# Score products of two token groups issued together at every second step of an attention kernel

## The chip, the cores and the metric

The kernel runs on one core of a Trainium2 chip. Time is the device time of one execution, in microseconds (us); a kernel's time is the median of its runs.

## What is computed

The reference is one layer of a bidirectional encoder on x (1, 1024, 1024): neighbourhood attention with 16 heads of 64, a layer norm, a squared-ReLU MLP of width 4096 with a sigmoid-gated per-layer embedding, and a second layer norm, all in float32. Cut to what matters:

```python
def neighborhood_attention(x, w_qkv, rpb, w_o):          # 16 rows of 64 tokens, window 8 x 16
    qkv = (x @ w_qkv).reshape(bsz, rows, GRID_W, 3, NA_HEADS, HEAD_DIM)
    q, k, v = qkv[:, :, :, 0] * HEAD_DIM ** -0.5, qkv[:, :, :, 1], qkv[:, :, :, 2]
    def row_block(r):                                     # one row of queries, kh rows of keys
        s = jnp.einsum('bqhd,bakhd->bhqak', q_r, k_b)
        s = jnp.where(col_in[:, None, :], s + bias, -jnp.inf)
        return jnp.einsum('bhqak,bakhd->bqhd', jax.nn.softmax(s, axis=(-2, -1)), v_b)
    return jnp.moveaxis(lax.map(row_block, jnp.arange(rows)), 0, 1).reshape(bsz, seq, D_MODEL) @ w_o

x = layer_norm(DN_ALPHA * x + neighborhood_attention(x, ...), ln1_g, ln1_b)
hid = jnp.square(jax.nn.relu(x @ w_ff1))
ple = jax.nn.sigmoid(x @ w_ple_gate) * (p @ w_ple_proj)
x = layer_norm(DN_ALPHA * x + hid @ w_ff2 + ple, ln2_g, ln2_b)
```

## The kernel before

Every matrix product is made of three products of a high and a low part (`PASSES`), so operands exist twice, `hi` and `lo`. The high part is a copy by ScalarE (or GpSimd), the low part a subtraction by VectorE (or GpSimd).

The attention is staged by pairs of heads, eight pairs (`PAIRS`), each in 16 steps (`UNITS`): a step handles one unit, that is one head of the pair and one group of 128 tokens, with keys from two or three neighbouring groups (256 or 384 columns). TensorE's program is one hand-written order. At step g of the whole sequence (s = g mod 16 within its pair) it issues:

- the scores of unit s (`scores`, matmuls of L1835): K's high part, then K's low part, both against the same q, into one of two banks `score_ps[u % 2]`;
- the transposes of the probabilities of unit s - 2 (`turn_p`, L1819);
- products with V (`weigh_v`, L1858) for the unit of four steps earlier; some steps have none, some two groups;
- six projection products (`project`, L1719), which make Q and K of the pair after. A projection group has 24 products and K's two groups come before Q's two. They run nearly a pair ahead, so the last pair has them only in its steps 0 and 1; from there embedding products (L1895) and transpositions of p (L1877) are spread over its steps.

The other engines follow in lists with the same g, strictly in order. VectorE's round: evacuations held over (last pair only), `add_bias` (L1542 and L1543: score + bias, negated, with the row's extreme; it frees the score bank through `score_done`), `turned_tile` of unit g - 3 (L1524, low part of the transposed probabilities, counter `turned_lo`), `out_sum` (L1555), `evac` (L1428 for Q, L1432 for K: the low parts of a finished projection), and `invert_total` (L1549), which waits for ScalarE's exponential of the same unit. ScalarE's round: `softmax_exp` (L1252), `turned_tile` of unit g - 2 (L1243), `out_low` (L1259), `evac` (L1167). GpSimd multiplies the probabilities by the reciprocal (`normalise`, L1054) and splits weights.

K has to stand twice in the partitions. When VectorE's last low part of K is done (in its round 12), SyncE, which waits for that count, issues four DMAs (`k_twice`, L778) that copy each half to the other 64 partitions. The first scores of the next pair wait for all four (`k_doubled`), and for the first part of Q (`proj_free`). The waits of `scores`:

```python
if u == 0:
    pe.wait_ge(k_doubled, 64 * j + 128)
...
pe.wait_ge(score_done, UNITS * j + (u + 1))
```

`score_done` starts at 2, so unit u waits for the bias pass of unit u - 2. The very first scores are issued ahead of the step loop, in the last of V's products (`v_product(4)`, L1753), once two banks that V's tiles used are free (`v_lo`, counted by L1503).

Of the kernel before, what the change touches and what calls it, by code (L numbers as in the profile page):

```python
# [20 lines left out]
P = 128  # L21
# [4 lines left out]
PAIRS = HEADS // 2  # L26
# [4 lines left out]
GROUPS = T // P  # L31
# [24 lines left out]
UNITS = 2 * GROUPS  # L56
# [6 lines left out]
FILL = PAIR_GROUPS * GROUP_MMS  # L63
STEP_FILL = FILL // UNITS
LAG = 2
AHEAD = FILL - LAG * STEP_FILL
# [12 lines left out]
QUARTER = GROUPS // 2  # L79
# [27 lines left out]
def blocks_of(g):  # L107

    return [d for d in (-1, 0, 1) if 0 <= g + d < GROUPS]
# [296 lines left out]
def attention(nc, S, x, w_qkv, rpb, mask, w_o, p, w_proj, ln_g, ln_b, w_gate):  # L406
# [5 lines left out]
    with ExitStack() as ctx:  # L412
        def sb(name, shape, dt=F32):
            return ctx.enter_context(nc.sbuf_tensor(name, shape, dt))

        def sem(name):
            return ctx.enter_context(nc.semaphore(name))
# [4 lines left out]
        q_st = sb("q_hi_lo", [P, 2, 2, T], F32R)  # L422

        k_st = []
# [33 lines left out]
        score_full = sem("score_full")  # L458
        score_done = sem("score_done")
# [7 lines left out]
        v_lo = sem("v_lo_done")  # L467
# [109 lines left out]
        def w_parts(p, k):  # L577
            return V_PARTS.index((p, k)) + 1
# [4 lines left out]
        def x_sum_parts(p, k):  # L583
            return KC2 * V_SUMS.index(p) + k + 1
# [67 lines left out]
        def low_count(kind, jn, pieces=W_LOWS):  # L652

            return W_LOWS * (2 * jn + kind - 1) + pieces
# [72 lines left out]
        proj_ps, score_ps, tile_ps, out_ps = S.ps[0:2], S.ps[2:4], S.ps[4:6], S.ps[6:8]  # L727
# [978 lines left out]
        def _(pe):  # L1706
            def project(first, last):

                for m in range(first, last):
                    jn, gi, i = m // FILL, m % FILL // GROUP_MMS, m % GROUP_MMS  # L1710
                    kind, t = gi // 2, gi % 2
                    k, (wp, ap) = i // len(PASSES), PASSES[i % len(PASSES)]
                    if i == 0:
                        pe.wait_ge(proj_free, 2 * PAIR_GROUPS * jn + (2 * gi + 2))
                    if jn == 0 and i == 0:
                        pe.wait_ge(w_lo, low_count(Q_, 0))
                    elif jn and t == 0 and i % (GROUP_MMS // W_LOWS) == 0:
                        pe.wait_ge(w_lo, low_count(kind, jn, i * W_LOWS // GROUP_MMS + 1))
                    mm = nc.tensor.matmul(proj_ps[gi % 2][:, :], w[wp][:, kind, k, :],  # L1719
                                          S.act[ap][:, k, t * HALF:(t + 1) * HALF],  # L1720
                                          start=(i == 0), stop=(i == GROUP_MMS - 1))
                    if i == GROUP_MMS - 1:
                        mm.then_inc(proj_full, 1)
# [65 lines left out]
            def v_product(p):  # L1789

                for k, i in [(2 * n + m, i) for n in range(KC2 // 2) for i in range(QUARTER) for m in range(2)]:
                    if p == 4 and (k, i) == (KC2 // 2, QUARTER - 1):
                        pe.wait_ge(v_lo, 2 * QUARTER + 2)
                        scores(0, 0, 0)
                    if i == 0:
                        pe.wait_ge(first_lo, w_parts(p, k))
                        if p in V_SUMS:
                            pe.wait_ge(t_lo, x_sum_parts(p, k))
                    if k == 0:
                        if p == 5:  # L1800
                            if i:
                                pe.wait_ge(proj_free, 4 + 2 * i)
                            else:
                                pe.wait_ge(x3_sum, X_SUMS_3)
                        elif p == 6:
                            pe.wait_ge(v_lo, i + 1)
                        elif p == 4:
                            pe.wait_ge(v_sum, QUARTER + i + 1)
                        else:
                            pe.wait_ge(v_copied, QUARTER * {3: 1, 7: 2}[p] + i + 1)  # L1810
                    v_products(p, i, k)

            def turn_p(j, u):
                pe.wait_ge(prob_ready, UNITS * j + (u + 1))
                pe.wait_ge(turned_lo, UNITS * j + (u + 1))
                if j == 0 and u < 2:
                    pe.wait_ge(v_lo, 3 * QUARTER + u + 1)
                for i in range(len(blocks_of(u % GROUPS))):
                    mm = nc.tensor.transpose(tile_ps[u % 2][:, i * P:(i + 1) * P],  # L1819
                                             prob[:, u % 4, i * P:(i + 1) * P], S.ident[:, :])  # L1820
                mm.then_inc(turned, 1)

            def scores(par, j, u):
                h, g = u // GROUPS, u % GROUPS
                keys = blocks_of(g)
                cols = slice((g + keys[0]) * P, (g + keys[-1] + 1) * P)
                if u == 0:
                    pe.wait_ge(k_doubled, 64 * j + 128)
                if j == 0 and u == GROUPS // 2 - 1:
                    pe.wait_ge(k_second_in, 16 + 64)  # L1830
                if g % (GROUPS // 2) == 0:
                    pe.wait_ge(proj_free, 2 * PAIR_GROUPS * j + (2 * (2 + g // 4) + h + 1 + 4))
                pe.wait_ge(score_done, UNITS * j + (u + 1))
                for part in range(2):
                    mm = nc.tensor.matmul(score_ps[u % 2][:, 0:P * len(keys)], q_st[:, par, h, g * P:(g + 1) * P],  # L1835
                                          k_st[part][:, par, h, cols], start=(part == 0), stop=(part == 1))
                mm.then_inc(score_full, 1)

            def weigh_v(par, j, nth, h, k):

# [104 lines left out]
            for p in V_PRODUCTS[2:]:  # L1945
                v_product(p)
# [4 lines left out]
            for g in range(STEPS):  # L1951
                j, s = divmod(g, UNITS)
                last = g - UNITS * LAST
                if 0 < g < PAIRS * UNITS:
                    scores(j % 2, j, s)
                if 0 <= g - TURN < PAIRS * UNITS:
                    turn_p(*divmod(g - TURN, UNITS))
                for jo, so in pairs_at(g):
                    for h, k in pv_units_at(so):
                        weigh_v(jo % 2, jo, jo // 2, h, k)  # L1960
                project(min(AHEAD + STEP_FILL * g, PAIRS * FILL), min(AHEAD + STEP_FILL * (g + 1), PAIRS * FILL))
                for u in embeds_at(last):
                    embed(u)
                for n in p_turns_at(last):
                    turn_p_rows(n)
                if last in EARLY_PRODUCTS:
                    done = sum(EARLY_PRODUCTS[i] for i in EARLY_PRODUCTS if i < last)
                    early_products(0, done, done + EARLY_PRODUCTS[last])
# [1391 lines left out]
```

## Time and profile before

| | us |
|---|---|
| median of 3 runs | 1212.5 (1211.63 to 1212.59) |
| the profiled execution | 1212.18 |
| its span | 1210.4 |
| TensorE busy | 1198.8 |
| VectorE busy | 860.4 |
| ScalarE busy | 614.6 |

In the rows below times are microseconds, in a timeline measured from the span's start. PE is TensorE's matmul queue, PEld its weight loads, DVE is VectorE, ACT ScalarE, POOL GpSimd, SPq the DMA issues of SyncE; L1835 is line 1835 of the kernel. A matmul's record starts where it enters the array and is longer than its share of the stream, so the distance from one start to the next is what it costs. In brackets stand the idle time ahead of an instruction and what ended it, inferred from semaphores; "issue" is time for which the profile shows no releaser.

### The profile page before, as it was taken

How to read it: one execution, taken by the hardware profiler on the slowest of the kernel's cores; microseconds unless marked ns; L12 is line 12 of the kernel's file. 1: busy time of each engine (PE TensorE's matmuls, PEld its weight loads, DVE VectorE, ACT ScalarE, POOL GpSimd, SP SyncE). 2: the span in 40 equal slices, each digit the busy share in tenths (PEclk: the TensorE clock that was granted, in tenths of full speed). 3: DMA queues.
4: the chain of work that ended last, by engine and by line, in shares of the span. 5: the costliest groups of instructions: out<-in, count | busy, mean ns of one | idle time of the engine just before them, and what ended most of it. 6: DMA issues, size and time to landing. Idle time of an engine off the chain costs nothing.

```text
span 1210.4 us, 17064 instructions
## 1 busy us (share of the span) xinstructions
PE 1198.8 (99%) x5708; PEld 1004.1 (83%) x5708; DVE 860.4 (71%) x1659; ACT 614.6 (51%) x1194; POOL 214.4 (18%) x262
## 2 busy tenths in 40 slices
PE   9999999999999999999999999999999999999997
PEld 7888888888887888888888888888888888888886
DVE  5785666666667668679677777677764565688786
ACT  5654676767767614244444444444454433333571
POOL 1312555555554424100000000000000000000000
PEclk9999999999999999999999999999999999999999
DMA  9669543344444977593555647566579785778533
GB/s 283 179 191 296 141 111 92 77 126 112 110 128 122 293 207 203 179 330 99 201 202 203 228 173 243 184 216 218 181 273 362 278 292 195 278 241 307 182 105 105
DMA packets 172134, 240.46 MB, mean 199 GB/s; under 512 B 12048, under 2 KB 93072, under 8 KB 171664
## 3 DMA queue, kind: packets, MB, share of 16 engines
q1 hardware_dynamic: 170848, 237.14, 59.9%
q0 software_dynamic: 1056, 2.10, 1.0%
q8 instruction: 47, 0.77, 0.3%
q14 instruction: 39, 0.32, 0.1%
q10 hardware_dynamic: 144, 0.13, 0.0%
HBM read 163.17 MB, written 68.87 MB: 192 GB/s over the span
## 4 chain that ended last, share of the span: by engine, by line
PE 94%; DMA 2%; DVE 2%; issue 1%; ACT 1%; SPq 0%; DVEq 0%; ACTq 0%
PE bank L3304 25%; PE bank L3272 25%; PE bank L1719 12%; PE bank L1902 7%; PE bank L3228 6%; PE bank L1753 5%; PE bank L1858 3%; PE bank L1835 3%; PE bank L1819 3%; PE bank L1783 1%; PE bank L1895 1%; DMA ple_embedding<-embedding_place 1%; DMA v_parts<-v_tile_parts 1%; PE bank L331 1%; DMA k_lo_twice<-k_lo_twice 0%
## 5 line engine op out<-in xcount | busy, mean ns | idle before, releaser
L1054 POOL TENSOR_TENSOR probabilities<-probabilities,total_reciprocal 128x384 f32<-128x384 f32 (+1 forms) x128 | 99.0, 774 | 156.6 <-DVE total_reciprocal L1549 156.5
L3272 PE MATMUL bank<-x_combination,weight_parts 128*128 128x512 f32 x504 | 118.5, 389 | 0.0
L1252 ACT ACTIVATE probabilities<-negated_scores,negated_max 128x384 f32<-128x384 f32 (+1 forms) x128 | 75.5, 590 | 82.3 <-DVE negated_max L1543 82.2
L3272 PEld LDWEIGHTS bank<-x_combination,weight_parts 128*128 128x128 f32 x504 | 94.6, 188 | 19.6
L1719 PE MATMUL bank<-act_T_hi,w_qkv_hi 128*128 128x512 f32 x232 | 93.3, 402 | 0.0
L1719 PE MATMUL bank<-act_T_lo,w_qkv_hi 128*128 128x512 f32 x232 | 91.1, 393 | 0.0
L1719 PE MATMUL bank<-act_T_hi,w_qkv_lo 128*128 128x512 f32 x232 | 91.1, 393 | 0.0
L1543 DVE CUSTOM_DVE_ANT_0 negated_scores<-bank,bias_inner 128x384 f32<-128x384 f32 x96 | 53.2, 554 | 47.8 <-issue 47.3
L2630 ACT ACTIVATE hidden_staging<-hidden_staging 128x512 f32<-128x512 f32 x48 | 30.4, 632 | 95.0 <-DVE hidden_staging L2970 95.0
L3272 PE MATMUL bank<-act_T_hi,weight_parts 128*128 128x512 f32 x240 | 77.3, 389 | 0.0
L3304 PE MATMUL bank<-x_combination,hidden_parts_odd 128*128 128x512 f32 (+1 forms) x324 | 73.1, 381 | 0.0
L3304 PE MATMUL bank<-x_combination,weight_parts 128*128 128x512 f32 x312 | 73.0, 389 | 0.0
L3304 PE MATMUL bank<-w_ff_parts,weight_parts_early 128*128 128x512 f32 x312 | 73.0, 389 | 0.0
L3304 PE MATMUL bank<-w_ff_parts,weight_parts 128*128 128x512 f32 x312 | 73.0, 389 | 0.0
L3304 PEld LDWEIGHTS bank<-x_combination,hidden_parts_odd 128*128 128x128 f32 x324 | 59.3, 188 | 11.8
L1524 DVE TENSOR_TENSOR prob_T_lo<-bank,prob_T_hi 128x256 fp32r<-128x256 f32 (+2 forms) x160 | 68.5, 445 | 0.2 <-ACT prob_T_hi L1243 0.2
L3304 PEld LDWEIGHTS bank<-w_ff_parts,weight_parts 128*128 128x128 f32 x312 | 58.6, 188 | 12.2
L3304 PEld LDWEIGHTS bank<-w_ff_parts,weight_parts_early 128*128 128x128 f32 x312 | 58.6, 188 | 12.1
L3304 PEld LDWEIGHTS bank<-x_combination,weight_parts 128*128 128x128 f32 x312 | 58.6, 188 | 12.1
L1243 ACT ACTIVATE prob_T_hi<-bank 128x256 fp32r<-128x256 f32 (+2 forms) x160 | 60.0, 396 | 2.2 <-PE bank L1858 0.9
L1819 PE MATMUL bank<-identity,probabilities 128*128 128x128 f32 x352 | 59.4, 272 | 0.4 <-DVE prob_T_lo L1524 0.4
L2769 DVE TENSOR_TENSOR weight_parts<-weight_raw,weight_parts 128x512 fp32r<-128x512 f32 x51 | 35.1, 690 | 34.4 <-ACT weight_parts L2539 34.4
(296 smaller groups left out, 2985.1 us busy)
## 6 DMA issues: line engine op xcount, KB each, us to landing
hidden_combinations<-hidden_staging SPq DMA_DIRECT2D x112, 256.0 KB, 2.3
w_ff_in<-in_w_ff SPq DMA_DIRECT2D x27, 1024.0 KB, 8.2
weight_raw<-in_w_ff SPq DMA_DIRECT2D x25, 1024.0 KB, 5.4
weight_raw<-hidden_combinations SPq DMA_DIRECT2D x14, 1024.0 KB, 5.5
hidden_in<-hidden_combinations SPq DMA_DIRECT2D x14, 1024.0 KB, 5.9
v_parts<-v_tile_parts SPq DMA_DIRECT2D x16, 512.0 KB, 7.9
v_hi_lo<-v_parts SPq DMA_DIRECT2D x8, 1024.0 KB, 6.7
weight_raw<-in_na_w_qkv SPq DMA_DIRECT2D x14, 512.0 KB, 3.9
```

The source lines that it names most:

```text
L1054: nc.gpsimd.tensor_tensor(prob[:, u % 4, 0:n], prob[:, u % 4, 0:n], recip[:, u % 4:u % 4 + 1].to_broadcast([P, n]), ALU.mult).then_inc(pro ...
L1243: last = nc.scalar.activation(pT_part(pT[0], g, first, count), tile_ps[u % 2][:, at * P:(at + count) * P].rearrange("p (b q) -> p b q", b= ...
L1252: nc.scalar.activation(prob[:, u % 4, 0:n], score[:, u % 2, 0:n], ACT.Exp, scale=-1.0, bias=nmax[:, u % 4:u % 4 + 1], accum_out=total[:, u ...
L1524: last = nc.vector.tensor_tensor(pT_part(pT[1], g, first, count), tile_ps[u % 2][:, at * P:(at + count) * P].rearrange("p (b q) -> p b q", ...
L1543: nc.vector.tensor_tensor_reduce(out=score[:, u % 2, 0:n], in0=score_ps[u % 2][:, 0:n], in1=table, scale=-1.0, scalar=3e38, op0=ALU.add, o ...
L1719: mm = nc.tensor.matmul(proj_ps[gi % 2][:, :], w[wp][:, kind, k, :], S.act[ap][:, k, t * HALF:(t + 1) * HALF], start=(i == 0), stop=(i == ...
L1753: mm = nc.tensor.matmul(bank, x_part[p](ap, k)[:, i * P:(i + 1) * P], (w_high(p), w_low[p])[wp][:, k, :], start=(p in (1, 6, 5) and k == 0 ...
L1819: mm = nc.tensor.transpose(tile_ps[u % 2][:, i * P:(i + 1) * P], prob[:, u % 4, i * P:(i + 1) * P], S.ident[:, :])
L1902: mm = nc.tensor.matmul(S.ps[2 * par + h][:, :], tile(ap, k), wo(wp, k)[:, h * HALF:(h + 1) * HALF], start=(k == 0 and n == 0), stop=(k == ...
L3228: mm = nc.tensor.matmul(bank, x, weights, start=(k == 0 and i == 0 and p in (1, 5, 6)), stop=(k == KH4 - 1 and i == 2), skip_group_check=p ...
L3272: mm = nc.tensor.matmul(bank, w1_part(wp, u, p)[:, k, :], x_part(ap, p, k), start=(k == 0 and n == 0 and p in (1, 5, 6)), stop=(k == KH4 - ...
L3304: mm = nc.tensor.matmul(bank, hid_part(ap, n, t)[:, k, :], weights(wp)[:, k, :], start=(start and k == 0 and i == 0), stop=(stop and k == ...
```

## The change

Scores of two units are issued together, at even steps, as four matmuls: high part of K for the first and the second unit, then low part for the first and the second. The counter `score_full` rises by 2 behind the fourth. They wait for both score banks (`score_done` at u + 2, so the bias pass of unit u - 1). The wait for the second half of the first pair's K stands one step earlier (u of 2 instead of 3). The first group, ahead of the loop, now holds units 0 and 1 and waits for one more tile of V. Projections are dealt out five at even and seven at odd steps instead of six at each. The other engines' programs are unchanged.

```diff
--- before.py
+++ after.py
@@ -1790,8 +1790,8 @@
 
                 for k, i in [(2 * n + m, i) for n in range(KC2 // 2) for i in range(QUARTER) for m in range(2)]:
                     if p == 4 and (k, i) == (KC2 // 2, QUARTER - 1):
-                        pe.wait_ge(v_lo, 2 * QUARTER + 2)
-                        scores(0, 0, 0)
+                        pe.wait_ge(v_lo, 2 * QUARTER + 3)
+                        scores_of_two(0, 0, 0)
                     if i == 0:
                         pe.wait_ge(first_lo, w_parts(p, k))
                         if p in V_SUMS:
@@ -1820,21 +1820,23 @@
                                              prob[:, u % 4, i * P:(i + 1) * P], S.ident[:, :])
                 mm.then_inc(turned, 1)
 
-            def scores(par, j, u):
+            def scores_of_two(par, j, u):
+
                 h, g = u // GROUPS, u % GROUPS
-                keys = blocks_of(g)
-                cols = slice((g + keys[0]) * P, (g + keys[-1] + 1) * P)
                 if u == 0:
                     pe.wait_ge(k_doubled, 64 * j + 128)
-                if j == 0 and u == GROUPS // 2 - 1:
+                if j == 0 and u == GROUPS // 2 - 2:
                     pe.wait_ge(k_second_in, 16 + 64)
                 if g % (GROUPS // 2) == 0:
                     pe.wait_ge(proj_free, 2 * PAIR_GROUPS * j + (2 * (2 + g // 4) + h + 1 + 4))
-                pe.wait_ge(score_done, UNITS * j + (u + 1))
+                pe.wait_ge(score_done, UNITS * j + (u + 2))
                 for part in range(2):
-                    mm = nc.tensor.matmul(score_ps[u % 2][:, 0:P * len(keys)], q_st[:, par, h, g * P:(g + 1) * P],
-                                          k_st[part][:, par, h, cols], start=(part == 0), stop=(part == 1))
-                mm.then_inc(score_full, 1)
+                    for b in range(2):
+                        keys = blocks_of(g + b)
+                        cols = slice((g + b + keys[0]) * P, (g + b + keys[-1] + 1) * P)
+                        mm = nc.tensor.matmul(score_ps[b][:, 0:P * len(keys)], q_st[:, par, h, (g + b) * P:(g + b + 1) * P],
+                                              k_st[part][:, par, h, cols], start=(part == 0), stop=(part == 1))
+                mm.then_inc(score_full, 2)
 
             def weigh_v(par, j, nth, h, k):
 
@@ -1951,14 +1953,14 @@
             for g in range(STEPS):
                 j, s = divmod(g, UNITS)
                 last = g - UNITS * LAST
-                if 0 < g < PAIRS * UNITS:
-                    scores(j % 2, j, s)
+                if g % 2 == 0 and 0 < g < PAIRS * UNITS:
+                    scores_of_two(j % 2, j, s)
                 if 0 <= g - TURN < PAIRS * UNITS:
                     turn_p(*divmod(g - TURN, UNITS))
                 for jo, so in pairs_at(g):
                     for h, k in pv_units_at(so):
                         weigh_v(jo % 2, jo, jo // 2, h, k)
-                project(min(AHEAD + STEP_FILL * g, PAIRS * FILL), min(AHEAD + STEP_FILL * (g + 1), PAIRS * FILL))
+                project(*(min(AHEAD + STEP_FILL * n - n % 2, PAIRS * FILL) for n in (g, g + 1)))
                 for u in embeds_at(last):
                     embed(u)
                 for n in p_turns_at(last):
```

## Rows read from the trace of the kernel before

**Rows 1.** The page, part 1: busy time, share of the span, instructions.

```profile
PE 1198.8 (99%) x5708; PEld 1004.1 (83%) x5708; DVE 860.4 (71%) x1659; ACT 614.6 (51%) x1194; POOL 214.4 (18%) x262
```

**Rows 2.** Stretches: length, busy time per engine, granted clock, DMA share.

```profile
188.00:226.00 38.00, 38.00 (x215) 33.22 (x214) 26.31 (x99) 26.45 (x69) 20.77 (x28) 1.00 0.38 103
...
374.00:398.00 24.00, 22.57 (x130) 18.48 (x130) 19.93 (x61) 18.15 (x44) 10.44 (x15) 1.00 0.40 137
```

**Rows 3.** Line L1835: idle time of its queues until a releaser (us, times).

```profile
  DMA k_lo_twice<-k_lo_twice: 2.5, 8
  DVE q_hi_lo L1428: 1.4, 3
```

**Rows 4.** Timeline of PE, step 12 of pair 2: start, us, engine, line, operation.

```profile
213.11 0.33 PE L1835 MATMUL bank<-k_hi_twice,q_hi_lo 128*128 128x384 f32 x1
213.28 0.33 PE L1835 MATMUL bank<-k_lo_twice,q_hi_lo 128*128 128x384 f32 x1
...
215.17 0.34 PE L1835 MATMUL bank<-k_hi_twice,q_hi_lo 128*128 128x384 f32 x1
```

**Rows 5.** Timeline of VectorE in the same step (idle time before in brackets).

```profile
213.66 0.56 DVE L1543 CUSTOM_DVE_ANT_0 negated_scores<-bank,bias_inner 128x384 f32<-128x384 f32 x1 [1.11 <-issue]
...
214.13 0.55 DVE L1524 TENSOR_TENSOR prob_T_lo<-bank,prob_T_hi 128x384 fp32r<-128x384 f32 x1
214.72 0.69 DVE L1432 TENSOR_TENSOR k_lo_twice<-bank,k_hi_twice 64x512 fp32r<-64x512 f32 x1
```

**Rows 6.** Timeline of SyncE: first and last of the four doubling DMAs.

```profile
215.44 0.47 SPq L778 DMA_DIRECT2D k_hi_twice<-k_hi_twice  x1
...
217.24 1.18 SPq L778 DMA_DIRECT2D k_lo_twice<-k_lo_twice  x1
```

**Rows 7.** Transfers of K's low part: 215 to 223 us, then the whole kernel.

```profile
DMA to landing us min/median/max: 3.8/4.4/4.9
...
DMA to landing us min/median/max: 3.6/4.5/7.5
```

**Rows 8.** Timeline of PE and its weight loads where pair 3 begins.

```profile
221.96 0.39 PE L1719 MATMUL bank<-act_T_hi,w_qkv_lo 128*128 128x512 f32 x1
...
222.18 0.19 PEld L1835 LDWEIGHTS bank<-k_hi_twice,q_hi_lo 128*128 128x128 f32 x1 [0.26 <-DMA k_lo_twice<-k_lo_twice]
222.19 0.39 PE L1835 MATMUL bank<-k_hi_twice,q_hi_lo 128*128 128x256 f32 x1
...
222.41 0.28 PE L1835 MATMUL bank<-k_lo_twice,q_hi_lo 128*128 128x256 f32 x1
```

**Rows 9.** Timeline of VectorE and PE in steps 1 to 4 of the last pair.

```profile
377.83 0.06 DVE L1542 MEMSET spare<- 128x1 f32 x1 [1.01 <-PE bank L1835]
...
380.67 0.55 DVE L1543 CUSTOM_DVE_ANT_0 negated_scores<-bank,bias_inner 128x384 f32<-128x384 f32 x1
...
383.23 0.55 DVE L1543 CUSTOM_DVE_ANT_0 negated_scores<-bank,bias_inner 128x384 f32<-128x384 f32 x1
383.25 0.44 PE L1835 MATMUL bank<-k_hi_twice,q_hi_lo 128*128 128x384 f32 x1 [0.40 <-DVE q_hi_lo L1428]
```

**Rows 10.** The same timeline: the third and the fourth transposition of p.

```profile
392.49 0.60 PE L1877 MATMUL bank<-identity,weight_raw 128*128 128x128 f32 x4
...
394.35 0.63 PE L1877 MATMUL bank<-identity,weight_raw 128*128 128x128 f32 x4 [0.35 <-ACT embedding_place L1280]
```

**Rows 11.** Timeline of VectorE: low parts of V's tiles 8 to 11.

```profile
98.01 2.47 DVE L1503 TENSOR_TENSOR v_tile_parts<-bank,v_tile_parts 128x512 fp32r<-128x512 f32 x4
```

**Rows 12.** Timeline around step 4 of the first pair.

```profile
117.60 0.68 DVE L1428 SCALAR_TENSOR_TENSOR q_hi_lo<-bank,q_hi_lo 64x512 fp32r<-64x512 f32 x1
...
118.33 0.19 PEld L1835 LDWEIGHTS bank<-k_hi_twice,q_hi_lo 128*128 128x128 f32 x1 [0.43 <-DVE q_hi_lo L1428]
```

**Rows 13.** The chain that ended last: products in turn, then in one bank.

```profile
16.33 1.82 PE bank L1753 x8
...
68.39 38.50 PE bank L1753 x168
```

## What the change was expected to do, and why

> **What bounds the kernel now.** The page's busy line comes first: TensorE is busy for 1198.8 us of a span of 1210.4 [rows 1], so only two things can move the time: work of TensorE, or the few places where it waits. The change adds and removes no matmul; it moves score products (L1835) and projection products (L1719). It acts on eight pairs of heads, each a run of 16 steps, between 107 and 425 us. The stretch views say how full these are: in 188 to 226 us TensorE has no idle time at a granted clock of 1.00, with VectorE busy 26.3 of 38 us; in 374 to 398 us, where no projections are left as filler, it is busy 22.57 of 24 [rows 2]. The next question is which wait ends last at the few places where TensorE waits. For the scores' line the source view names two: the DMA that doubles K (2.5 us, 8 times) and VectorE's low part of Q (1.4 us, 3 times) [rows 3]. Both are idle times of the weight-load and matmul queues together; part of each is hidden.
>
> **The K path, which decides.** I follow it in the pair that starts at 222.18 us; six other pair starts (146.54, 184.36, 259.97, 297.92, 336.12, 373.97) look the same. Step 12 of the pair before begins at 213.11 with two score matmuls 0.17 us apart [rows 4]. VectorE waits for them, starts the bias pass at 213.66 (0.55 after the step's start, 0.38 after the second matmul's), runs the low part of the transposed tile (214.13 to 214.68) and only then the last low part of K, 214.72 to 215.41 [rows 5]. The bias row shows 1.11 us idle before it: what holds VectorE here is the scores, not a backlog. SyncE issues the first doubling DMA at 215.44 and the fourth at 217.24 [rows 6]; the slowest lands 4.9 us after issue [rows 7], so at 222.14. The weight load of pair 3's first score starts at 222.18, named as waiting 0.26 us for that DMA, and its matmul needs 0.22 us to the next where columns alone (256) need 0.12 [rows 8]. So K arrives late by a hair today: the load should start with the last projection at 221.96. There is no cushion; whatever delays K's low part delays TensorE one for one.
>
> **Parts of the change.**
>
> (a) Four score matmuls at each even step instead of two at each step. Columns and loads are the same. A 384-column matmul takes 0.17 us of the stream [rows 4]. The counter rises once, behind the fourth, so for an even unit VectorE starts at 3 x 0.174 + 0.38 = 0.90 us after the step's start instead of 0.55: **0.35 later**. Queued behind that bias pass on VectorE are the tile's low part, the evacuations of K and Q and the reciprocal; ScalarE's exponential waits for it too.
>
> (b) Of that, step 12 matters: the last K part ends at 213.11 + 2.30 + 0.35, the DMAs are issued and land 0.35 later, TensorE's own path from step 12 to step 0 holds the same products as before and so still takes 9.08 (213.11 to 222.19). Stall: 0.35 per pair start. Six starts inside the full stretch: 6 x 0.35 = **+2.1**. The seventh (373.97) goes into (e). Bounds: 0 per start if the landing time were set by something other than issue; 0.6 if the landing is in a bad slot (over the whole kernel K's low transfers land 3.6 to 7.5 us after issue, median 4.5 [rows 7]). I take 0.35, the row's own value.
>
> (c) Odd units are ready about 2 us sooner. VectorE can't use all of it: the bias pass of unit 13 stands behind the reciprocal of unit 12, which stands behind that unit's exponential. No one waits for odd units in the full steps, so 0.
>
> (d) Odd steps now open with transposes (L1819), and TensorE must find `turned_lo` of the tile three units back. In step 12, the shortest (2.06 us, 213.11 to 215.17 [rows 4]), the step becomes 2.06 + 0.35 - 0.23 = 2.18; the load of the first transpose wants to start at 1.95; VectorE's low part ends at 1.57 + 0.35 = 1.92 [rows 5]. It just fits. Cost 0, bounds 0 and 0.05 for each short step (two a pair, 16 in all): up to +0.8. The longer steps (2.3 to 2.6) have 0.2 us or more. The new condition on both score banks (`score_done` of unit u - 1) is met about 0.9 us ahead, since that bias pass now runs in the middle of the odd step; 0. Of the 5-and-7 split: group borders fall on even steps and stay where they are, the `w_lo` waits are for pieces finished some three steps before; 0.
>
> (e) The last pair. Without projections VectorE's queue is the bound from 377.8 to 384.3. Today it idles 1.01 us at 377.83 waiting for the score of step 1 [rows 9]; with that score there from step 0 this goes. But the gain is not kept: at step 2 it must wait for four score matmuls (the step starts at 379.68 today, about 380.0 behind the seventh K stall; + 0.9 = 380.9, against 380.67 today [rows 9]). From there it works without a break as before (380.67 to 383.23, 2.56 us), 0.2 to 0.3 later: bias of unit 3 from 383.5. Step 4's scores today start at 383.25, on VectorE's low part of Q [rows 9]; after, they also need the bias pass of unit 3 done, at about 384.0, and are four. What follows them, the transposes held by `prob_T_lo`, ends up 0.2 to 0.3 later than now. At step 7 the second transposition of p comes 1.86 us after the first (392.49, 394.35 [rows 10]), held by ScalarE; the scores that fill part of that gap today (0.23 us) move in front of it. Sum of the last pair, its own K stall included: **+0.4**, bounds -1.0 (the 1.01 is kept) and +1.2.
>
> (f) Start. The first group is now two units and waits for one more freed bank (`v_lo` 11, not 10). The four low parts n = 8 to 11 are one block from 98.01 to 100.48 [rows 11], over 6 us before TensorE gets there: 0. Unit 1's score leaves step 1. At step 4 of the first pair the load waited 0.43 us for Q's low part, 117.60 to 118.28 [rows 12]; its bias pass belongs to the odd unit 3, whose score now comes with step 2, so that part ends near 118.0: **-0.2**, bounds -0.3 and 0.
>
> (g) Alternating banks inside a group of scores. The chain has both patterns for 512 columns: 8 products into four banks in turn in 1.82 us (0.228 each), 168 mostly into one bank in 38.50 (0.229) [rows 13]. No difference; 256 matmuls x +-0.002 is +-0.5.
>
> **Sum** against the profiled execution's own 1212.18 (span 1210.4 and 1.8 around it): 2.1 + 0.4 - 0.2 = +2.3, so 1214.5. The median of the runs shown is 1212.5, 0.3 above that execution: **1214.8**.
>
> **The skill against the rows.** The fourth K transfer takes 4.9 us from issue to landing [rows 7]. The Trainium skill (DMA: Bandwidth & Descriptors, Anatomy of one DMA) gives, for another issue path, some 2.0 us plus bytes over 436 GB/s. For 256 KB that is an estimate of 2.6 us from that page; K would then land near 219.8, the delay of 0.35 would be free and the sum +0.2. The trace does not bear it out here. Second, the granted clock is 1.00 in a stretch whose products already go round eight banks [rows 2]. The Trainium skill (TensorE: Matmul & The Clock Gate, A second HAM failure mode: psum-queue depth-cycling) says that cycling through PSUM banks can make the clock swing between its levels. By that rule more alternation would cost time; the trace speaks against it.
>
> **Rivals.**
> - *K is not late* (15%): the doubling's landing follows its slot in the DMA queues, not its issue, or TensorE's path between steps 12 and 0 grows by itself. For: landing times vary [rows 7]. Against: in seven pairs load start and landing agree within 0.1 us. Then the sum is +0.2: 1212.7.
> - *Odd steps wait* (10%): the fit in (d) fails. Mechanism: VectorE's low part, 0.35 late in every even round, is needed at the head of the next step, where the two scores used to stand in between. It decides once VectorE's round is more than 0.05 us later than I have it. Price: 0.1 us at 56 odd steps is 5.6 on top of the forecast less its last pair: about 1220. For: 0.03 us of margin in the short steps. Against: longer steps have 0.2 us and more.
> - *Faster* (10%): the change does what its order promises. VectorE keeps the 1.01 us in the last pair, K lands in good slots and even the 0.1 us exposed at each of the seven starts goes, and half the score waits at step heads disappear at some 0.02 us each in 64 steps: -1.0 - 0.7 - 0.2 - 1.3 = -3.2, 1209.3. Against: steps with scores at their head show no gap today [rows 4].
>
> **Chances.** Forecast 65%, by itself 1213.3 to 1216.4. Faster and slower are counted beyond 0.2% (2.4 us, about what a measurement of this kernel tells from no change), so the forecast stands on the upper bound, 1214.9, and splits in halves: same 0.33 and slower 0.32. "K not late" adds 0.12 to same and 0.03 to faster; "odd steps" 0.10 to slower; "faster" 0.07 to faster and 0.03 to same. Together 0.10, 0.48, 0.42. The range leaves out most of the odd-step case and of the faster one: 1211.5 to 1217.2.
>
> **What will show it.** Right: at the seven pair starts the load's wait for K's DMA is some 0.6 us instead of 0.26, the step-12 bias pass starts 0.90 after its step, and a full pair takes 38.2 us instead of 37.8. The odd steps open without a gap; VectorE's wait at step 1 of the last pair is gone, a new one stands at step 2. Wrong: pair starts unchanged, pairs no longer than 37.8, or gaps in front of L1819 at odd steps.

## The result, and the profile after

The changed kernel takes 1216.41 us (median of 10 runs) against 1212.55 for the kernel before on the same chip: a ratio of 1.0032, 95% interval 1.0022 to 1.0042. That is 3.9 us, **slower by 0.3%**. The forecast was 1214.8, with 1211.5 to 1217.2 as its range: the time is inside the range, 1.6 above the forecast and at the upper end of the 1213.3 to 1216.4 that the forecast case had by itself. The sign, which stood on the edge of the 0.2% bound, came out on the slower side; the prediction had given 0.48 to "same" and 0.42 to "slower". One execution of the repeat of the changed kernel (below) took 3123.69 us, for a reason that the record doesn't show; it is left out of that kernel's figures.

The page's busy line, which answers to [rows 1]:

```profile
span 1214.4 us, 17064 instructions
PE 1199.9 (99%) x5708; PEld 1003.8 (83%) x5708; DVE 857.7 (71%) x1659; ACT 612.7 (50%) x1194; POOL 214.3 (18%) x262
```

The counts of instructions are those of before; the span grew by 4.0 us and busy TensorE by 1.1. The two stretches of [rows 2], moved by 1 and 3 us, roughly with the work they hold (length, busy time of PE, PEld, DVE, ACT and POOL, granted clock, DMA share, GB/s):

```profile
189.00:227.00 38.00, 37.82 (x212) 32.77 (x212) 25.57 (x97) 25.90 (x69) 20.55 (x28) 1.00 0.39 103
377.00:401.00 24.00, 21.49 (x127) 18.07 (x127) 18.46 (x60) 17.81 (x44) 10.45 (x15) 1.00 0.38 122
```

The clock is 1.00 as before. Idle time has appeared in the full stretch, the pairs in which projections fill every step (38.00 busy before, 37.82 now), and 1.1 us more of it in the last pair (22.57, now 21.49), 0.23 of that at the pair's start. Which wait it is, the view by line shows, first the scores' line (L1837 now, L1835 before), answering to [rows 3]:

```profile
its engine sat idle before it (us, times) until:
  DMA k_lo_twice<-k_lo_twice: 7.1, 14
  DVE q_hi_lo L1428: 1.6, 2
  DVE negated_max L1543: 1.1, 1
```

The DMA that doubles K went from 2.5 us to 7.1, the sum of both queues. Seven of the 14 are weight loads, 5.0 us of it; in the kernel before they came to 2.4.

The K path through the same pair as in [rows 4 to 8], timelines of PE, its weight loads, VectorE and SyncE (start, us, engine, line, operation, idle time before it):

```profile
214.66 0.51 PE L1837 MATMUL bank<-k_hi_twice,q_hi_lo 128*128 128x384 f32 x2
215.01 0.52 PE L1837 MATMUL bank<-k_lo_twice,q_hi_lo 128*128 128x384 f32 x2
...
215.57 0.55 DVE L1543 CUSTOM_DVE_ANT_0 negated_scores<-bank,bias_inner 128x384 f32<-128x384 f32 x1 [1.90 <-issue]
216.05 0.55 DVE L1524 TENSOR_TENSOR prob_T_lo<-bank,prob_T_hi 128x384 fp32r<-128x384 f32 x1
216.63 0.70 DVE L1432 TENSOR_TENSOR k_lo_twice<-bank,k_hi_twice 64x512 fp32r<-64x512 f32 x1
...
217.36 0.47 SPq L778 DMA_DIRECT2D k_hi_twice<-k_hi_twice  x1
...
219.16 1.18 SPq L778 DMA_DIRECT2D k_lo_twice<-k_lo_twice  x1
...
DMA to landing us min/median/max: 3.8/4.3/4.9
...
223.52 0.39 PE L1719 MATMUL bank<-act_T_hi,w_qkv_lo 128*128 128x512 f32 x1
224.09 0.30 PEld L1837 LDWEIGHTS bank<-k_hi_twice,q_hi_lo 128*128 128x128 f32 x2 [0.61 <-DMA k_lo_twice<-k_lo_twice]
224.09 0.56 PE L1837 MATMUL bank<-k_hi_twice,q_hi_lo 128*128 128x256 f32 x2 [0.18 <-DMA k_lo_twice<-k_lo_twice]
```

Read from the step's start: the bias pass begins 0.91 us in (215.57 less 214.66) where it began 0.55 in, K's last low part 1.97 in instead of 1.61, SyncE's first doubling DMA 2.70 instead of 2.33, the fourth 4.50 instead of 4.13. The landing takes 4.9 us from issue as before, and TensorE's weight load, behind a last projection that started at 223.52, waits 0.61 us where it waited 0.26. The matmul queue itself stands still for 0.18 of that. The whole way is 0.36 longer from end to end.

**Where the time went**, by the starts of the steps in the profiled execution (1216.21 us, against 1212.18 of before): 0.8 us had been lost ahead of the first score (107.52, against 106.73), where the two programs are the same but for one more tile of V that is waited for; 2.7 at the seven pair starts (+0.42, 0.41, 0.34, 0.33, 0.45, 0.34 and 0.37 at the start itself; step 4 of the first pair gave 0.12 back, and the other steps of the full stretch differ by 0.06 or less); 0.4 to 0.5 in the last pair, from its step 0 to its step 14 (40.68, now 41.13); 0.1 behind it. These are one execution of each kernel; what a second pair of executions makes of them stands in the part on why.

### The profile page after: what moved, and what is told of

Its sections match the earlier page's. It is cut to its first block, busy times and chain, and to the rows that moved or that the text cites. A ratio compares the mean times of both kernels' runs of the same rounds, so it can differ in the third digit from the quotient of the medians.

```text
span 1214.4 us, 17064 instructions
## 1 busy us (share of the span) xinstructions
PE 1199.9 (99%) x5708; PEld 1003.8 (83%) x5708; DVE 857.7 (71%) x1659; ACT 612.7 (50%) x1194; POOL 214.3 (18%) x262
## 4 chain that ended last, share of the span: by engine, by line
PE 83%; issue 5%; DMA 5%; DVE 4%; SPq 1%; ACT 1%; DVEq 0%; ACTq 0%
PE bank L3306 25%; PE bank L3274 25%; PE bank L1904 7%; PE bank L3230 6%; PE bank L1753 6%; PE bank L1719 6%; DMA k_lo_twice<-k_lo_twice 3%; PE bank L1837 2%; PE bank L1860 2%; PE bank L1819 1%; PE bank L1783 1%; DMA ple_embedding<-embedding_place 1%; DVE prob_T_lo L1524 1%; SPq L778 1%; DVE k_lo_twice L1432 1%
## 5 line engine op out<-in xcount | busy, mean ns | idle before, releaser
L1819 PE MATMUL bank<-identity,probabilities 128*128 128x128 f32 x352 | 59.4, 272 | 0.5 <-POOL probabilities L1054 0.3
```

## Experiments

Each kernel's runs stand beside runs of the kernel before on the same chip (their medians were 1212.55 to 1213.09; the ratios are against those of the same chip). Times of steps are from the profiled execution, counted from the first score's start in it, so that the scatter ahead of it (below) stays out. "Seven starts" is the start of the last pair, "last pair" the time from its step 0 to its step 14, "K wait" what the weight loads at the pair starts waited for the doubling DMA, sum and longest. A ratio of medians on different chips is not used; differences in us between kernels of different chips are good to about the 0.5 us by which the medians of the kernel before differ.

| kernel | median us | ratio to before, 95% | seven starts | last pair | K wait, longest |
|---|---|---|---|---|---|
| before | 1212.55 | | 267.24 | 40.68 | 2.4, 0.6 |
| before again | 1212.40 | 0.9996 (0.9987 to 1.0005) | 267.43 | 41.85 | 2.6, 0.5 |
| after | 1216.41 | 1.0032 (1.0022 to 1.0042) | 269.91 | 41.13 | 5.0, 0.9 |
| after again | 1215.99 | 1.0028 (1.0016 to 1.0039) | 271.44 | 40.79 | 6.5, 1.6 |
| e1, step 12 unit by unit | 1213.04 | 1.0003 (0.9994 to 1.0012) | 267.28 | 40.78 | 2.6, 0.6 |
| e2, all steps unit by unit | 1212.16 | 0.9994 (0.9985 to 1.0003) | 267.48 | 40.13 | 3.0, 0.7 |
| e4, before, step-12 scores late | 1215.86 | 1.0028 (1.0018 to 1.0038) | 270.40 | 41.18 | 5.7, 1.1 |
| e5, after, K's low part first | 1211.21 | 0.9990 (0.9981 to 0.9999) | 266.06 | 40.66 | none |
| e6, before, K's low part first | 1211.47 | 0.9989 (0.9981 to 0.9998) | 266.18 | 41.63 | none |
| e8, after, six and six | 1215.85 | 1.0025 (1.0013 to 1.0036) | 271.03 | 40.62 | 6.4, 1.6 |
| e9, e2 and K's low part first | 1210.46 | 0.9983 (0.9974 to 0.9992) | 265.69 | 40.31 | none |
| e10, after, last pair in single units | 1214.80 | 1.0018 (1.0009 to 1.0027) | 269.84 | 41.47 | 5.0, 0.9 |

**The theory** is the forecast's: the bias pass of step 12 stands ahead of K's last low part on VectorE, so what delays its scores delays K and TensorE, one for one. **The rivals**: K's landing doesn't follow its issue and the time comes from elsewhere; and the order of banks, the odd steps or the five-and-seven split cost TensorE time by themselves.

### Step 12 alone, unit by unit (e1)

The even unit's two matmuls come first again, with a rise of the counter of their own, in step 12 only; the four stay in one group.

```
-                for part in range(2):
-                    for b in range(2):
+                early = u == 12
+                for part, b in ([(0, 0), (1, 0), (0, 1), (1, 1)] if early else [(0, 0), (0, 1), (1, 0), (1, 1)]):
...
-                mm.then_inc(score_full, 2)
+                    if part == 1 and (early or b):
+                        mm.then_inc(score_full, 1 if early else 2)
```

> The changed kernel, but in step 12 of each pair alone the four score matmuls go both parts of the first unit, then both of the second, and the counter rises by one behind each unit; the work is the same. Theory K (what the change costs is the 0.35 us by which the step-12 bias pass, and with it K's low part and its doubling DMAs, come later): the seven pair starts go back to where they were, 7 x 0.38 = 2.7 us gained on the changed kernel, so about 1.0 us above before (1213.6); the load at a pair's start waits about 0.26 us for K's DMA again. Rival O (the loss comes from odd steps that open with transposes, or from the order of the four matmuls in general): 7 of 64 groups change, at most 0.3 us gained, 1216.1.

Measured 1213.04 (ratio 1.0003), 3.4 us less than the change. The pair starts are those of the kernel before again (267.28 and 267.24), and so is the wait for K:

```profile
213.60 0.55 DVE L1543 CUSTOM_DVE_ANT_0 negated_scores<-bank,bias_inner 128x384 f32<-128x384 f32 x1 [1.54 <-issue]
...
214.67 0.69 DVE L1432 TENSOR_TENSOR k_lo_twice<-bank,k_hi_twice 64x512 fp32r<-64x512 f32 x1
...
PEld bank L1837 <- DMA k_lo_twice<-k_lo_twice: 2.6, 7, 0.6
```

The step starts at 213.05: the bias pass is back at 0.55, K's part at 1.62. One step in sixteen, and only the order and the signal of four matmuls in it, holds nearly all of the change's cost. The gain is larger than the 2.7 expected; 2.6 of it stands at the seven starts.

### Every group unit by unit (e2)

The same edit with `early = True`: what is left of the change is the grouping of two units, one bank after the other, and the split.

> The changed kernel, but every pair of score products goes unit by unit, the counter rising behind each unit; the order 'K's high part first for both' is gone everywhere. Theory K: as the run with step 12 alone, 2.7 us gained on the changed kernel, and in the last pair, where VectorE's round is the bound, up to 0.3 more: about 1213.4. Rival (alternating the banks is worth something on TensorE): slower than the run with step 12 alone, by up to 0.5 us.

Measured 1212.16 (0.9994, the interval holds 1), 1.2 below the 1213.4 expected. Against e1 the seven pairs are 0.2 longer and the last pair 0.65 shorter, where up to 0.3 was expected. So the grouping of two units and the split cost nothing, and going round the banks inside a group, which e1 still does in seven of a pair's eight groups and e2 in none, makes no difference in the full pairs that these runs can tell.

### The kernel before with its step-12 scores behind two projections (e4)

This brings the delay into the kernel before, with nothing else of the change.

```
+                ahead = 2 if s == 12 and j < LAST else 0
+                project(AHEAD + STEP_FILL * g, AHEAD + STEP_FILL * g + ahead)
                 if 0 < g < PAIRS * UNITS:
                     scores(j % 2, j, s)
...
-                project(min(AHEAD + STEP_FILL * g, PAIRS * FILL), min(AHEAD + STEP_FILL * (g + 1), PAIRS * FILL))
+                project(min(AHEAD + STEP_FILL * g + ahead, PAIRS * FILL), min(AHEAD + STEP_FILL * (g + 1), PAIRS * FILL))
```

> The kernel before, with one thing moved: in step 12 of each of the first seven pairs two of the six projection products go ahead of the scores instead of behind them. No pairing, no new wait. The step-12 bias pass starts 2 x 0.23 = 0.46 us later. Theory K: 7 x 0.46 = 3.2 us slower than before, 1215.8, all of it at pair starts. Rival (the landing of K's doubling follows the DMA queues, not its issue, or the loss is in the pairing itself): within 0.5 us of before.

Measured 1215.86 (1.0028), and +3.16 us over the seven starts (expected 3.2). K's landing does follow its issue (6.7 to 7.1 us from SyncE's first issue to the load, at all seven starts): the rival falls. At the start that answers to [rows 8]:

```profile
223.42 0.19 PEld L1835 LDWEIGHTS bank<-k_hi_twice,q_hi_lo 128*128 128x128 f32 x1 [0.74 <-DMA k_lo_twice<-k_lo_twice]
...
PEld bank L1835 <- DMA k_lo_twice<-k_lo_twice: 5.7, 7, 1.1
```

The wait grew from 0.26 to 0.74, which is the 0.46 by which two projection products (2 x 0.23) hold the scores back.

### K's last low part ahead of the bias pass (e5, e6, e9)

The other way round: in VectorE's round 12 the evacuation that stood behind the bias pass, and behind the tile's low part, goes in front of both. e5 does it to the changed kernel, e6 to the kernel before, e9 to e2.

```
                     for which in evacs_before(g - 1):
                         evac(*which)
+                    if s == 12:
+                        for which in evacs_behind(g - 1):
+                            evac(*which)
...
-                if g:
+                if g and s != 12:
                     for which in evacs_behind(g - 1):
                         evac(*which)
```

> The changed kernel, with VectorE's last low part of K put ahead of the bias pass in its round 12 (ScalarE's half of it is done by then, 0.2 us after the step's start), so that the doubling DMAs go out some 1.7 us sooner than in the changed kernel. Theory K: the stalls at pair starts vanish altogether, 7 x (0.38 + about 0.1) = 3.4 us gained on the changed kernel: 1213.0, and no wait of a weight load for K's DMA is left. Rival O: at most 0.5 us gained, 1216.

> The kernel before, unpaired, with VectorE's last low part of K ahead of the bias pass in round 12. Theory K: the landing moves some 1.0 us ahead of its need, so all pairs come down to the 37.75 us seen once K was early in the changed kernel; the pair starts of before then gain 267.24 - 266.06 = 1.2 us: 1211.4. Rival (pairing by itself is worth time once K is out of the way): this kernel stays over 1 us above the changed kernel with K's low part first (1211.2), at 1212.3 or more.

> Scores issued two units at a time, but unit by unit with the counter rising behind each, and K's low part first in round 12. Theory K plus the last pair's share: pairs of 37.75 us as with K's low part first alone, and the last pair 0.5 us shorter, as in the run that went unit by unit everywhere: 1210.7. Rival (the two gains are the same one): 1211.2 or above.

e5 measured 1211.21, 5.2 us less than the change where 3.4 was expected, and 0.1% faster than the kernel before (the interval ends at 0.9999). By the profiled executions 3.85 of the gain stands at the seven starts, 0.5 in the last pair and 1.1 ahead of the first score, which the edit doesn't touch: the last of these is scatter. In e5, step 12 starts at 212.35 and pair 3 at 221.45:

```profile
212.13 0.69 DVE L1432 TENSOR_TENSOR k_lo_twice<-bank,k_hi_twice 64x512 fp32r<-64x512 f32 x1 [0.78 <-ACT k_hi_twice L1167]
...
212.85 0.47 SPq L778 DMA_DIRECT2D k_hi_twice<-k_hi_twice  x1
...
213.35 0.56 DVE L1543 CUSTOM_DVE_ANT_0 negated_scores<-bank,bias_inner 128x384 f32<-128x384 f32 x1
...
221.22 0.39 PE L1722 MATMUL bank<-act_T_hi,w_qkv_lo 128*128 128x512 f32 x1
221.45 0.45 PE L1840 MATMUL bank<-k_hi_twice,q_hi_lo 128*128 128x256 f32 x2
```

K's part waits for ScalarE alone and begins 0.22 us ahead of the step; the doubling DMAs follow at 212.85, and at 221.45 the score products come 0.23 behind the last projection, with no wait. All pairs from the second on take 37.75 us. The order of the change is still in it (four scores, then the bias pass), and in the full steps it costs no more than the 0.03 us a pair by which e9, below, is shorter.

e6 shows the same with the kernel before: pairs of 37.71 to 37.78 us from the second on, 1211.47 (0.9989), as expected (1211.4). Its last pair took 0.95 longer, most of it a wait of 0.82 for the embedding. e9 is the best of all, 1210.46 us (1210.7 expected), 0.9983 (0.9974 to 0.9992): by that ratio it beats the kernel before by 2.1 us, and by the medians the change by 6.0, with every pair from the second to the seventh at 37.72 us.

### The split at six and six (e8)

```
-                project(*(min(AHEAD + STEP_FILL * n - n % 2, PAIRS * FILL) for n in (g, g + 1)))
+                project(min(AHEAD + STEP_FILL * g, PAIRS * FILL), min(AHEAD + STEP_FILL * (g + 1), PAIRS * FILL))
```

> The changed kernel with six projection products at every step, as before. Even steps get 0.23 us longer and odd ones shorter; the work is the same. Theory K: two even steps (12 and 14) lie between the step-12 scores and the next pair's start, and two odd ones, so TensorE's path does not change and the stalls stay: 1216.4 within 0.5. Rival O (odd steps wait for VectorE's low part at their head): longer even steps give it 0.23 us more, the time falls by up to 2 us.

Measured 1215.85 (1.0025), 0.6 below the change, at the edge of the 0.5 expected, with intervals that overlap. The pairs take 38.15, 38.20, 38.23 and 38.51 us where the changed kernel's take 38.22, 38.19, 38.26 and 38.52; two took longer, by a longer wait for K at the start behind them: the fifth 39.12 (38.37 in the change; a wait of 1.57), the first 40.63 (40.10; 1.34). The split of projections costs nothing and brings nothing that can be told apart.

### The last pair in single units (e10)

The steps of the last pair call the old `scores` at every step again; the seven pairs ahead of it stay as changed.

```
-                if g % 2 == 0 and 0 < g < PAIRS * UNITS:
+                if j == LAST:
+                    scores(j % 2, j, s)
+                elif g % 2 == 0 and 0 < g < PAIRS * UNITS:
                     scores_of_two(j % 2, j, s)
```

> The changed kernel, but the last pair issues its scores one unit a step, as before. Theory of the prediction (the last pair loses 0.4 us by pairing, since VectorE waits for four matmuls at step 2 and TensorE for a second bias pass at step 4): 0.45 us off the changed kernel, 1215.9, and the last pair's steps 0 to 14 take 40.7 us, not 41.1. Rival (the last pair's loss is a late echo of its late start): 1216.4, steps 0 to 14 stay at 41.1.

Measured 1214.80, 1.6 below the change where 0.45 was expected; the two ratio intervals still overlap. By its steps the last pair goes as in the kernel before up to step 10 (28.38 us from its start; before 28.40, change 28.77): a gain of 0.39. Then this execution waited for the embedding, and steps 0 to 14 took 41.47 us, not the 40.7 expected and not less than the change's 41.13:

```profile
PE bank L1913 <- ACT embedding_place L1280: 0.8, 1, 0.8
```

So the loss of 0.4 up to step 10 is shown to come from the grouping in the last pair. That the last pair as a whole is shorter without the grouping is not shown, and the 1.6 is not located.

**This wait goes with the order of the last pair.** It stands in front of the embedding products some 33 us into the pair. In the repeat of the kernel before (e12) it reads, with ScalarE's copy that TensorE waits for and the store whose landing that copy waits for:

```profile
407.49 0.60 ACT L1280 ACTIVATE embedding_place<-bank 128x512 f32<-128x512 f32 x1 [4.59 <-DMA ple_embedding<-embedding_place]
...
408.14 0.50 PE L1895 MATMUL bank<-act_T_hi 128*128 128x512 f32 x1 [1.11 <-ACT embedding_place L1280]
```

Five of the twelve traces have a last pair in single units: TensorE waits there in four (0.39 in e4, 0.76 in e10, 0.82 in e6, 1.11 in e12) and not in the first execution of the kernel before. Seven have it in groups of two, and none has the wait. So the 40.68 of the first execution is the kernel before at its best: single units take 40.7 to 41.9, the change's order 40.6 to 41.1, unit by unit in groups of two 40.1 to 40.3. Why the store lands later in the one order was not tried.

### Both kernels once more

The change had lost 0.8 us ahead of the first score, where its program is that of before. Does that belong to it?

> The changed kernel once more, unchanged, to see how far the 0.8 us that its profiled execution lost ahead of the first scores (107.52 us, against 106.73 in the kernel before, with the same program up to there) belongs to it or to that one execution. If it belongs to the one execution: first scores between 106.2 and 107.0, the seven pair starts again at some 269.9 us and the last at some 41.1 us behind them, so a median near 1215.7, 3.1 above the kernel before. If something in the changed kernel's program costs it each time: first scores again near 107.5 and 1216.4, 3.9 above.

> The kernel before once more, as a kernel of its own against its own runs, on the same chip: the ratio should be 1.000 within 0.001; the first scores' start in a second profiled execution (106.73 in the first) shows the scatter of the stretch ahead of them, expected within 0.5 us; pair starts 267.2 and last pair 40.7 again within 0.3.

It doesn't: this time the changed kernel's first score comes at 106.99 and the kernel before's at 107.45 (0.7 from its first execution, where 0.5 was expected). Still the changed kernel takes 1215.99 against 1213.09 on that chip, a ratio of 1.0028, and the kernel before against its own runs has 0.9996. The total came out as expected for this case (1215.7, 3.1 above), but not by the parts expected: the seven starts stand at 271.44 and not at 269.9, 4.0 us above the kernel before (267.43), and the last pair of the kernel before took 41.85 where 40.7 was expected, so the change's 40.79 is 1.1 shorter. At the starts:

```profile
147.87 0.30 PEld L1837 LDWEIGHTS bank<-k_hi_twice,q_hi_lo 128*128 128x128 f32 x2 [1.56 <-DMA k_lo_twice<-k_lo_twice]
...
262.91 0.30 PEld L1837 LDWEIGHTS bank<-k_hi_twice,q_hi_lo 128*128 128x128 f32 x2 [1.07 <-DMA k_lo_twice<-k_lo_twice]
301.63 0.30 PEld L1837 LDWEIGHTS bank<-k_hi_twice,q_hi_lo 128*128 128x128 f32 x2 [1.11 <-DMA k_lo_twice<-k_lo_twice]
...
PEld bank L1837 <- DMA k_lo_twice<-k_lo_twice: 6.5, 7, 1.6
```

The other four waits are 0.58 to 0.93, as in the first execution. Ahead of the load at 262.91, SyncE's issues read:

```profile
255.71 0.47 SPq L778 DMA_DIRECT2D k_hi_twice<-k_hi_twice  x1
256.23 1.64 SPq L778 DMA_DIRECT2D k_lo_twice<-k_lo_twice  x1
257.91 0.60 SPq L778 DMA_DIRECT2D k_hi_twice<-k_hi_twice  x1
258.55 0.61 SPq L778 DMA_DIRECT2D k_lo_twice<-k_lo_twice  x1
```

One of the four issues is long each time; mostly it is the last, with no issue behind it that it could hold up (1.18 at 219.16). Here it is the second, and from the first issue to the load it takes 7.20 us (255.71 to 262.91) instead of the 6.73 of 217.36 to 224.09. It was the second once in the kernel before too (1.36 us) and the third once (1.96), but the way from first issue to load was 6.87 and 6.83 there. Ahead of the wait of 1.56 the four issues were as usual (140.19 to 142.05), and still the load came 7.68 us behind the first.

## Why the prediction came out as it did

- **The K path (b)** is right in place and mechanism. 0.91 for the bias pass (0.90 forecast), 0.36 late at the issue (0.35), the load's wait 0.61 (some 0.6), full pairs of 38.2 to 38.5 (38.2). e1 takes the delay away and 3.4 us go; e4 brings one in and 3.2 come. What was off is the **size of the term**: "I take 0.35, the row's own value". Over two executions each, the loads waited 11.5 us in 14 starts with the change and 5.0 before, 0.46 more per start and 3.3 per run instead of 2.45. An ordinary start costs 0.24 to 0.45, and now and then one costs 0.4 to 0.7 more, because K takes longer from SyncE's first issue: over 7.1 us at 3 of the 14 starts in the two executions of the change and at 2 of 7 in e8 (7.43, 7.67), never over 7.07 in the 14 of the kernel before, nor in the 14 of e4 and e10, which issue as late as the change. I had both ends of that (0 to 0.6 "if the landing is in a bad slot") and took the row of one start as the mean of all; the seven starts don't "look the same": in the kernel before their loads wait 0.23 to 0.58.
- **The last pair (e)**, +0.4 with its K stall of 0.35 included, leaves 0.05 for the pair's own steps. In the first pair of executions they cost 0.45, in the second the change is 1.1 shorter. By the traces the change's order costs 0.1 to 0.4 up to step 10 (28.6 to 28.8 us, single units 28.4 to 28.5), and as much or more was given back in four of five comparisons by the wait for the embedding that the single units have. That the whole term is near its forecast in one comparison is luck: the path that decides it, the embedding's store, is not in the prediction. Two lines went as forecast, the gain at step 1 and its loss at step 2; two things cost more:

```profile
380.58 0.63 PE L1879 MATMUL bank<-identity,weight_raw 128*128 128x128 f32 x4 [0.35 <-DVE q_hi_lo L1428]
...
380.67 0.56 DVE L1543 CUSTOM_DVE_ANT_0 negated_scores<-bank,bias_inner 128x384 f32<-128x384 f32 x1
...
384.26 0.55 DVE L1543 CUSTOM_DVE_ANT_0 negated_scores<-bank,bias_inner 128x384 f32<-128x384 f32 x1 [0.76 <-issue]
...
386.82 0.55 DVE L1543 CUSTOM_DVE_ANT_0 negated_scores<-bank,bias_inner 128x384 f32<-128x384 f32 x1
387.52 0.59 PE L1837 MATMUL bank<-k_hi_twice,q_hi_lo 128*128 128x384 f32 x2 [1.12 <-DVE negated_max L1543]
...
398.18 0.63 PE L1879 MATMUL bank<-identity,weight_raw 128*128 128x128 f32 x4 [0.59 <-ACT embedding_place L1280]
```

  Against [rows 9], as forecast: no wait ahead of unit 1's bias pass (380.67), a new one of 0.76 ahead of unit 2's (384.26), and step 4's scores held by unit 3's bias pass (387.52). Not foreseen: the bias pass of unit 0 is late by 0.34 too, Q's low part stands behind it, and the transposition at the end of step 0 waits 0.35 for that (380.58). I had looked at step 2 and not at step 0, which already has this queue. The held scores of step 4, which were forecast, open at 10.09 us into the pair instead of 9.28, but only 0.14 of that 0.8 is left at step 6. Another 0.24 comes back in step 7: the transposition at 398.18 waits 0.59 for ScalarE where it waited 0.35 [rows 10], since the scores that filled part of that gap now stand in front of it. The prediction saw them move and put no cost on it. At step 8 the pair is 0.38 behind, at step 14 0.46.
- **Odd units (c), odd steps (d), the split, the start (f) and the banks (g).** TensorE has no gap in front of L1819 in the full steps, so the narrow fit in (d) held and the rival "odd steps wait" falls (the weight loads of that line stand idle for 11.5 us in all instead of 4.9, hidden behind running matmuls); step 4 of the first pair gained 0.12 (0.2 forecast); e2 and e8 confirm the zeros of (g) and the split.
- **"K is not late"** falls by e4. Its sum of +0.2 was also added up wrongly: the 0.4 of (e) still holds the seventh start's stall of 0.35, so by its own terms it is some -0.15. The Trainium skill (DMA: Bandwidth & Descriptors, Anatomy of one DMA) has a fit for another issue path, from which the prediction estimated 2.6 us for 256 KB. It does not carry over to these copies: the rows show 4.9. The Trainium skill's passage on cycling through PSUM banks (TensorE: Matmul & The Clock Gate, A second HAM failure mode: psum-queue depth-cycling) doesn't show either: the granted clock is 1.00 in the stretches of both kernels and in e2.
- **"Faster"** falls. Its third part, "the 0.1 us exposed at each of the seven starts", was there to be had, but by K's place on VectorE and not by the order of scores: with the wait gone, a pair takes 37.72 instead of 37.82 (e9, e5, e6).
- **The sum.** Forecast +2.3 over the profiled execution; measured +3.9 and, again, +2.9 between the medians of the second pair. Over the two profiled executions of each kernel the change is 3.4 us longer: 3.3 at the seven starts (2.7 and 4.0), -0.3 in the last pair (+0.45 and -1.1), 0.2 ahead of the first score (106.73 and 107.45 before, 107.52 and 106.99 after) and 0.2 behind step 14. The last three are no larger than what single executions scatter; the starts are the change's cost. A single execution agrees with the median of its kernel only to about 1.7 us, so how often a slow start occurs stays open; what makes one slow wasn't tried.

## What to carry to other kernels

When a transfer at the end of a chain lands just as its user needs it, look for what stands ahead of its producer in the queue of an in-order engine: here a bias pass that waits for another engine's result. One change of order on VectorE took the whole wait away (5.2 us off the changed kernel), more than the best order of the matmuls did (4.3, e2). Grouping products of two units under one signal delays the first unit's consumer by the products that now stand ahead of the signal (0.36 us here); keep the group but signal unit by unit. Cost a delay on such a path with the spread of the transfer's issue and landing over all its occurrences, not with the row of one: without a cushion the slow ones count in full. And take a second execution of the kernel before, too, before a few tenths of a microsecond are put down to the change: here the last pair's sign turned over with it.

## What was not expected of the hardware

The four doubling DMAs take 6.7 to 7.1 us from the first issue to the load that they release, but 7.2 to 7.7 at five starts: three of seven in one execution of the change, two of seven in e8, none in the other execution of the change nor in e4 and e10. All five are in kernels that issue them late (5 of 35 starts; none of the 28 of the kernel before, e1 and e2), but lateness is not what it takes. Where K's low part goes first, SyncE issues them earliest, and they are slower still in e5 and e9: by the traces' landing times the last one lands 6.8 to 8.2 us after the first issue there, 6.7 to 7.3 in e6, against 6.7 to 7.0 in the kernel before. In those kernels it costs nothing, because even so they land before the load needs them. In the kernel before and in the change the four land 1.2 to 1.5 us apart at the start followed above though they are issued 0.5 to 0.7 apart, so they do not run freely beside each other. What they share the time with, no run here tells.

Ahead of the first score, where the programs are the same but for one tile of V that is waited for, executions scatter widely: 106.99 to 108.26 in the three of the changed kernel and e8, 106.25 to 108.26 in all twelve. And the last pair waits 0.4 to 1.1 us for the embedding in four of five executions with single units and in none of seven with groups of two.
